# A linear-recurrence block on one core: the keys' transposes inside a half unit, and sums of squares by split products

## The reference, cut to what matters

```
q, log_f, k, v = heads of  h @ w_in          # f = lb + (1 - lb) * sigmoid(f_pre), k = 1 - f
o_inter = (q * exp(b)) @ state               # b = cumulated log_f within a chunk
o_intra = sum_s (q_t . k_s . exp(b_t - b_s)) v_s
state   = exp(b_last) * state + (k * exp(b_last - b))^T v
o       = o * rsqrt(mean(o * o) + eps) * hgrn_norm_w * silu(g)
```

## Time and profile before

| | |
|---|---|
| median of 3 runs | 2016.26 us (2016.15 to 2017.52) |
| profiled execution, its own time | 2014.99 us |
| its span | 2013.0 us |
| PE busy | 1957.5 us (97% of the span) |
| DVE busy | 1362.8 us (68%) |
| ACT busy | 825.1 us (41%) |
| POOL busy | 941.8 us (47%) |
| stretch of the recurrence | about 100 to 600 us |

### The profile page before, as it was taken

How to read it: one execution, slowest core, us unless ns; L and a number is a source line. 1 busy time by engine, 2 the same in 40 slices (tenths; PEclk the granted TensorE clock), 3 DMA queues, 4 the chain that set the end, 5 groups by cost and what they waited for, 6 DMA issues and landing times.

```text
span 2013.0 us, 28505 instructions
## 1 busy us (share of the span) xinstructions
PE 1957.5 (97%) x10565; PEld 1596.2 (79%) x10565; DVE 1362.8 (68%) x1816; ACT 825.1 (41%) x1313; POOL 941.8 (47%) x548
## 2 busy tenths in 40 slices
PE   7999999999999999999999899898999999999997
PEld 6887878888887768878888678677888888888886
DVE  7888777767638654786141487898856656667978
ACT  4444454344421024563300486566333333334453
POOL 1354465333334469742454110956655455445553
PEclk8999999999999999999999899999999999999999
DMA  9323222211112253133110200222433323356344
GB/s 281 81 82 119 73 73 104 94 31 31 53 55 58 67 176 127 45 145 117 50 44 11 84 2 1 74 105 100 131 93 95 124 85 104 105 188 240 102 139 168
DMA packets 179503, 194.01 MB, mean 96 GB/s; under 512 B 9863, under 2 KB 122968, under 8 KB 179418
## 3 DMA queue, kind: packets, MB, share of 16 engines
q1 hardware_dynamic: 172996, 178.53, 27.9%
q10 hardware_dynamic: 6422, 14.37, 2.0%
HBM read 151.71 MB, written 41.16 MB: 96 GB/s over the span
## 4 chain that ended last, share of the span: by engine, by line
PE 79%; DVE 10%; ACT 6%; issue 3%; POOL 1%; ACTq 0%; DVEq 0%; POOLq 0%
PE psum L1003 7%; PE psum L1563 7%; PE psum L1564 7%; PE psum L1565 7%; PE psum L1005 7%; PE psum L1004 7%; PE psum L1666 3%; PE psum L1667 3%; PE psum L1668 3%; PE psum L1023 3%; PE psum L1024 3%; PE psum L1025 3%; PE psum L1324 2%; PE psum L1326 2%; PE psum L1325 2%
## 5 line engine op out<-in xcount | busy, mean ns | idle before, releaser
L795 POOL TENSOR_TENSOR w_hi<-w_raw,ones 128x1024 fp32r<-128x1024 f32 x60 | 151.8, 2530 | 463.0 <-PE psum L1005 338.8
L1003 PE MATMUL psum<-h_hi,w_hi 128*128 128x512 f32 x704 | 284.4, 404 | 0.0
L1005 PE MATMUL psum<-h_hi,w_lo 128*128 128x512 f32 x704 | 274.7, 390 | 0.0
L1004 PE MATMUL psum<-h_lo,w_hi 128*128 128x512 f32 x704 | 274.3, 390 | 0.0
L798 POOL TENSOR_TENSOR w_lo<-w_raw,w_hi 128x1024 fp32r<-128x1024 f32 x60 | 165.7, 2761 | 4.7
L1698 ACT ACTIVATE arena<-psum 128x1024 f32<-128x1024 f32 (+7 forms) x103 | 80.4, 788 | 209.8 <-PE psum L1005 130.1
L1003 PEld LDWEIGHTS psum<-h_hi,w_hi 128*128 128x128 f32 x704 | 132.2, 188 | 29.4 <-issue 2.6
L1004 PEld LDWEIGHTS psum<-h_lo,w_hi 128*128 128x128 f32 x704 | 132.3, 188 | 28.4 <-issue 2.6
L1005 PEld LDWEIGHTS psum<-h_hi,w_lo 128*128 128x128 f32 x704 | 132.1, 188 | 28.3
L1666 PE MATMUL psum<-w_hi,h_hi 128*128 128x512 f32 x308 | 120.1, 390 | 3.1 <-DVE h_lo L3302 3.1
L993 POOL TENSOR_TENSOR w_lo<-arena,w_hi 128x512 fp32r<-128x512 f32 x61 | 86.3, 1419 | 75.5 <-ACT w_hi L1698 75.5
(11 more groups left out here) (491 smaller groups left out, 5183.6 us busy)
## 6 DMA issues: line engine op xcount, KB each, us to landing
w_raw<-w_in SPq DMA_DIRECT2D x64, 512.0 KB, 3.9
act_op<-arena SPq DMA_DIRECT2D x77, 256.0 KB, 2.3
arena<-act_op SPq DMA_DIRECT2D x77, 256.0 KB, 2.7
w_raw<-w_gate SPq DMA_DIRECT2D x22, 512.0 KB, 4.0
w_raw<-w_up SPq DMA_DIRECT2D x22, 512.0 KB, 5.2
arena<-ada_w SPq DMA_DIRECT2D x16, 512.0 KB, 7.2
arena<-w_out SPq DMA_DIRECT2D x16, 512.0 KB, 5.9
out_T<-arena SPq DMA_DIRECT2D x16, 512.0 KB, 5.4
```

The costliest lines, as they stand in the source:

```text
L1003: pe.matmul(o, wh, xh, start=(k == 0), stop=False)
L1004: pe.matmul(o, wh, xl, start=False, stop=False)
L1005: return pe.matmul(o, wl, xh, start=False, stop=(k == KT - 1))
```

## The change

The product with ones takes rounded operands. ScalarE squares twice, once into `sq_hi` (fp32r, in page `B_D[2]`) and once into page `B_SQ` (float32); VectorE subtracts (`squares_lo`) and writes `sq_lo` (fp32r, over `B_SQ`); PE multiplies `ones_r` by `sq_hi` and then by `sq_lo` into the same bank, four products of 512 columns in place of two in float32. `sq_done` counts three steps to a head in place of one. ScalarE's squares move ahead of the two `span_exp`. VectorE's subtraction stands between the keys' and the queries' product of `base_kq`, which is cut in two for it; for the last head it stands between two `window` calls. `task_t1` moves from before `z(1,1)` to within it, behind the fifth of its eight feature tiles. The same function bodies serve the passes in the loop and the ones written out.

```diff
-        ones = sb("ones", [P, P])
+        ones_r = sb("ones_r", [P, P], F32R)
+        ones = ones_r[:].bitcast(F32)
...
-            def fm_half(c, out, half):
+            def fm_half(c, out, half, within=None):
                 for k in range(KT):
                     mm = fm_k(c, out[:, half * HALF:(half + 1) * HALF], k, half)
+                    if within is not None and k == 4:
+                        within()
...
-                pe.wait_ge(sq_done, h + 1)
-                for half in range(2):
-                    mm = pe.matmul(psum[:, 4 + half, :], ones[:], page(B_SQ)[:, half * HALF:(half + 1) * HALF], start=True, stop=True)
+                for e, sq in enumerate((sq_hi, sq_lo)):
+                    pe.wait_ge(sq_done, 3 * h + (2 + e))
+                    for half in range(2):
+                        mm = pe.matmul(psum[:, 4 + half, :], ones_r[:], sq[:, half * HALF:(half + 1) * HALF], start=(e == 0), stop=(e == 1))
...
                 task_t0(h)
-                task_t1(h)
-                z(1, 1)
+                z(1, 1, lambda: task_t1(h))
...
                 base_exp(h)
+                if not (type(h) is int and h == 0):
+                    o_squares(h - 1)
                 span_exp(h, 0)
                 span_exp(h, 1)
-                if not (type(h) is int and h == 0):
-                    o_squares(h - 1)
...
                 act.wait_ge(task_full, TASKS * h + TASK_O)
+                A(sq_hi, two_banks(3), ACT.Square).then_inc(sq_done, 1)
                 A(page(B_SQ), two_banks(3), ACT.Square).then_inc(sq_done, 1)
...
+            def squares_lo(h):
+                dve.wait_ge(sq_done, 3 * h + 2)
+                TT(sq_lo, page(B_SQ), sq_hi.bitcast(F32), ALU.subtract).then_inc(sq_done, 1)
...
-                base_kq(h)
+                base_k(h)
+                if not (type(h) is int and h == 0):
+                    squares_lo(h - 1)
+                base_q(h)
                 span_kq(h, 0)
```

More of the change, by code:

```diff
@@ L321, in program @@
         first_raw_k = lambda s: (first_raw if s < 2 else w_raw)[:, s, :].rearrange("p (k c) -> p k c", c=P)
+        sq_hi, sq_lo = [rounded_pages(name, i, 1)[:] for name, i in (("sq_hi", B_D[2]), ("sq_lo", B_SQ))]
         gate_part = [page(GATE_W)[:, h * HALF:(h + 1) * HALF] for h in range(2)]
@@ L1251, in gate_rows, with z_half @@
                 mm.then_inc(mod_mm, 1)
-            def z_half(it, j, half):
+            def z_half(it, j, half, within=None):
                 if half == 0:
@@ L1259, in z_half @@
                     pe.wait_ge(w_ready, 4 * it + (j + 1))
-                mm = fm_half(j % 2, two_banks(j % 2), half)
+                mm = fm_half(j % 2, two_banks(j % 2), half, within)
                 if half:
                     mm.then_inc(w_used, 1)
-            head(0, lambda j, half: z_half(1, j, half))
+            head(0, lambda j, half, within=None: z_half(1, j, half, within))
             with pe.Fori(2, HEADS) as it:
-                head(it - 1, lambda j, half: z_half(it, j, half))
+                head(it - 1, lambda j, half, within=None: z_half(it, j, half, within))
             def pool_slot(g, j):
@@ L1298, in pool_mix, with pool_half @@
                     mm.then_inc(pm_full, 1)
-            def pool_half(j, half):
+            def pool_half(j, half, within=None):
                 if half == 0:
@@ L2570, in base_d, with base_k, base_q @@
                 STT(x.rearrange("p (n w) -> p n w", w=BASE), ref, -0.5, b4, ALU.mult, ALU.add).then_inc(d4_done, 1)
-            def base_kq(h):
+            def base_k(h):
                 dve.wait_ge(e4_done, 2 * h + 2)
                 TT(page(B_K4), page(B_K4), kk_, ALU.mult).then_inc(kq4_done, 1)
+            def base_q(h):
                 TT(page(B_Q4), page(B_Q4), qq, ALU.mult).then_inc(kq4_done, 1)
@@ L2748, in _ @@
             window(0, 0)
+            squares_lo(h)
             window(0, 1)
```

## The result

| | before | after |
|---|---|---|
| median | 2016.15 us (2015.14 to 2018.25, 9 runs) | 2022.27 us (2020.37 to 2024.86, 9 runs) |
| ratio | | 1.0029, 95% interval 1.002 to 1.0038 |
| profiled execution, its span | 2014.99, 2013.0 us | 2020.67, 2018.7 us |
| PE busy | 1957.5 us (97%) | 1955.4 us (97%) |
| DVE busy | 1362.8 us (68%) | 1398.6 us (69%) |

What follows compares the result with a forecast made beforehand. PE's own work bounds full passes; ScalarE's path, then VectorE's norm, sets slow ones. Profiled 2014.99 - 3.2 (products) + 4.1 (slow passes) = 2015.9; with the median 1.27 above the profiled execution, 2017.2 us; range 2005.5 to 2020.5.

Steps and rivals of the forecast that it cites:

- Part 1, the product with ones: Rounded products on PE save 0.80 us a product; four in full passes give -3.2 us.
- full pass: Pass over a head of 60.25 us in which PE is busy throughout; forecast near 59.45 us after the change.
- Part 2, the second square: Lengthens ScalarE's path to the norm by 0.95 us; PE waits 0 or 0.2 us at the first transposes.
- Part 3, the move: Keys' transposes behind five tiles give the norm 3.40 us more; PE arrives at 293.1; mixing product kinds costs nothing.
- slow pass: Pass of 61.96 us, PE busy 60.67, set by ScalarE, then VectorE's norm, then the keys' transposes; forecast 62.96 us.
- Part 4, the turns: VectorE's subtraction opens a 0.4 us gap, so GpSimd alternates with it; slow passes 1.0 us longer, four +4.1 us.
- two rows: Profile rows at 111.12 and 282.00 where GpSimd's L795 waits for VectorE's run to end; evidence for VectorE keeping its turns.
- the last of part 4: Slow pass: transposes start at 295.95, `task_base` 3.14 us later at 299.1 in place of 298.05.
- the first (VectorE keeps its turns, -9.8 us): Slow passes: GpSimd waits until `qe` times `q` is done, each 1.65 us shorter; 2006.5 us; at least one turn kept: 0.26.
- the forecast's case: VectorE and GpSimd alternate behind the subtraction in slow passes; 2017.2 us, own range 2014.7 to 2019.7; chance 0.60.
- The second rival: Slow passes: the subtraction comes behind GpSimd's L795, `task_base` 2.0 us later; +4.8, 2021.1 us; chance 0.08.
- The third: Product with ones: four rounded parts as slow as the plain ones, full passes gain nothing; +4.1, 2020.4 us; chance 0.02.

Runs made afterwards that it cites:

- subtraction first: Changed kernel with ScalarE's two squares ahead of its base exponentials and VectorE's subtraction ahead of the keys' product: 2017.7 us, ratio 1.0006.
- squares first: Changed kernel with ScalarE's two squares ahead of its two base exponentials, VectorE's order unchanged: 2027.56 us, ratio 1.0059.
- better version: Kernel before with the keys' transposes behind five tiles and its one square ahead of the base exponentials, no subtraction: 2009.68 us, ratio 0.9969.
- filler kernel: Changed kernel with eleven unread rounded products put ahead of TensorE's wait for the norm, in the loop's six passes: 2021.68 us in one run.

## Why the prediction was wrong, point by point

- **Part 1, the product with ones**: right. -0.84 us a full pass, forecast -0.80.
- **Part 2, the second square**: right in size; it stands on ScalarE's path and TensorE's wait at the first transposes is 0.2 us (0.5 us in the kernel without the subtraction). "Moving both squares ahead of the spans' exponentials costs nothing else" was wrong: in the kernel without the subtraction VectorE waits 0.17 us for the first of these exponentials, which lets GpSimd in. It did not show in the sum, since the subtraction's gap came first.
- **Part 3, the move**: right. TensorE began to wait at 296.91, on the clock of before 293.23, forecast 293.1; alone the move brings a slow pass from 61.96 to 60.7 us. Its price of nothing for transposes among rounded products held to 0.02 us.
- **Part 4, the turns**: right, place by place, to 0.1 us. The gap was 0.35 us (0.4 forecast) and the pass without the fall of the clock got 1.15 us longer (1.0 forecast). That the gap decides is borne out by the kernels that followed: with no gap VectorE kept the turn (subtraction behind the queries' product, subtraction first), with one some operations ahead it lost it (changed kernel, squares first, without subtraction; in the full passes of the changed kernel the gap lies four operations ahead of the one that loses, `qe` times `q`, 3.42 us). One of the "two rows" that "show VectorE keeping the turn" was misread: at 282.00 VectorE keeps one turn (L2584) and loses the next, since L2640 takes 3.37 us in place of 1.22. The better version shows what that turn hangs on. The Trainium skill (SBUF — State Buffer, Who interferes with whom) calls the shared ports an exclusive lock, which it says of VectorE's two-port modes is held for the whole instruction, and says that issue order decides who blocks. The alternation agrees with a lock for one instruction (2.88 us for an operation of 0.68); the 5.62 us of L797 across an unbroken run of VectorE's do not, so the rule gives the price of a turn, not who gets it.
- **The step that failed** is the last of part 4: "PE has waited there since 293.1 ... it begins at 295.95 + 3.14 = 299.1". The wait was priced at its own length and the 3.14 us behind it at full clock. They took 3.14 us in one pass, 4.71 and 4.75 in two, and in the first, where the clock fell later, 4.51 with the rest of the loss in `task_base`. With 3 x 1.58 us added to 2015.9 the sum is 2020.6 us against 2020.67 of the profiled execution (so close by luck: small misses of up to 0.5 us cancel in it); the other 0.3 of the 5.1 us is that the median lies 1.60 us above the profiled execution, where 1.27 was assumed. The filler kernel shows that this is the wait's doing. The price stood in no row of the recurrence of before, since the wait there was 1.1 us, and I had not looked for what a longer one does elsewhere: the stretch from 1133.51, shown with the result, has it.
- The Trainium skill has the rule, and it was not weighed: TensorE: Matmul & The Clock Gate, HAM oscillation — how this bites in real kernels, warns that a TensorE starved between pieces of work has its clock throttled and starts each next piece cold. The 64.67 us against 63.11 agree with it, and the fourth wait of 2.83 us, with no fall behind it, does not agree with "each"; the page's example has longer waits, for a DMA.
- **The rivals**: the first (VectorE keeps its turns, -9.8 us) has the right mechanism and a wrong price. The two kernels that realise it, the second of them in its first and third slow pass only, are at 2019.19 and 2017.7 us, since GpSimd's work, 2.3 us later at the start of the pass, meets the span products and the scans at its end. Had the forecast's case not come, the time would probably still not have been 2006.5; the changed kernel itself was not run in that case. The second rival (subtraction behind L797, 2021.1 us) lies near the result by accident: L797 came at 285.68, 0.9 us behind the start of the subtraction. The third did not happen.

What stays open: why the fall follows some waits of the same length and not others (two of four at 2.15 us, three of four at 2.83, one of three at 3.3). Also whether a version with the split and without either collision exists. The kernel without the subtraction, at 2003.96 us, shows at best what it would be worth, since it leaves that work out.

## What to carry to other kernels

A forecast wait of TensorE, where it sets the time, can have two prices: its length, and the slower clock on the work behind it. Look through the whole trace, and not only the stretch of the change, for a row with a wait of that length before adding it up, or give the engine less to wait for. Where two engines take turns at a shared resource, a wait put into one engine's queue can decide the turns of all that follows, and an engine that gains at the start of a loop body pays if its partner's displaced work meets a row of short operations at its end; follow the displaced work to the end of the pass before crediting a gain.

## What was not expected of the hardware

- Eleven useless products of 0.23 us in a wait of 2.8 us made the pass 1.6 us shorter.
- Eight short scans take 3.77 us with one of them behind the end of a GpSimd operation and 9.09 us with three. Each of the three turns costs a whole GpSimd operation, 2.15 us on top of a scan of 0.40.
- A difference of about 2 us in when VectorE comes to its four late span products (43.2 us into the pass without the subtraction, 45.1 with the subtraction first) makes 4 to 8 us in the next pass, which then loses it again or not, so that passes of one loop take 59.42 and 67.36 us by turns.
